# Sparse attention of a two-block transformer: four group turns become one unrolled stream of 64 steps

## The reference, cut to what matters

```python
def nsa_compressed(q, k, v, ...):      # 31 compressed keys and values per group
    s = einsum('bsghd,bngd->bghsn', q, kc) * NSA_SCALE
    p = masked_softmax(s, end[None, :] <= t[:, None])
    o = einsum('bghsn,bngd->bsghd', p, vc)
# selected blocks: top 16 of 8 blocks of 64 keys, so all of them, under the causal mask
# window: 512 keys back, with 512 tokens in all, so the causal mask alone
#   s = einsum(q, k) * NSA_SCALE ; p = masked_softmax(s, mask) ; o = einsum(p, v)
# the three outputs of a head are summed, each times its own gate per token and head
```

## Time and profile before

| | us |
|---|---|
| median of 3 runs (2740.66 to 2742.11) | 2741.51 |
| the profiled execution | 2737.46 |
| its span, first to last instruction | 2735.2 |
| PE busy | 2542.9 (93%) |
| POOL busy | 963.8 (35%) |
| ACT busy | 913.7 (33%) |
| DVE busy | 670.7 (25%) |
| sparse attention on PE, 1426.06 to 1798.09 | 372.0 |

### The profile page before, as it was taken

The page is one execution under the profiler, slowest core; times in us unless marked ns, Lnnn a source line. Parts: engine busy times, 40 slices in busy tenths (PEclk is TensorE's granted clock), DMA queues, the critical chain, the costliest instruction groups (busy, mean ns, idle before and its releaser), DMA issues.

```text
span 2735.2 us, 30881 instructions
## 1 busy us (share of the span) xinstructions
PE 2542.9 (93%) x11116; PEld 1937.5 (71%) x11116; DVE 670.7 (25%) x1619; ACT 913.7 (33%) x1579; POOL 963.8 (35%) x496
## 2 busy tenths in 40 slices
PE   6999999999899899999888888889799999899997
PEld 5888775766676688877576655657566667788776
DVE  1011211223232201121305345435521111301121
ACT  4322322345344333232313244333332223432232
POOL 3444452522523544445212210223322224244344
PEclk9999999999999999999967786889899999899999
DMA  3322234221111233223300100101112222123232
GB/s 130 99 93 92 87 106 140 88 66 62 62 54 61 70 93 99 92 85 102 114 22 29 35 27 8 35 31 54 39 48 91 81 86 89 57 94 100 77 97 89
DMA packets 72938, 204.00 MB, mean 75 GB/s; under 512 B 7185, under 2 KB 22033, under 8 KB 72337
## 3 DMA queue, kind: packets, MB, share of 16 engines
q1 hardware_dynamic: 69760, 191.92, 22.2%
q10 hardware_dynamic: 3088, 10.97, 1.1%
HBM read 199.71 MB, written 2.10 MB: 74 GB/s over the span
## 4 chain that ended last, share of the span: by engine, by line
PE 72%; issue 16%; DVE 5%; ACT 4%; POOL 3%; DMA 0%; DVEq 0%; ACTq 0%; POOLq 0%
PE bank L614 15%; PE bank L615 15%; PE bank L621 15%; PE bank L827 4%; PE bank L1047 3%; POOL parts L461 3%; PE bank L764 2%; PE bank L1267 1%; ACT parts L1526 1%; PE bank L660 1%; PE bank L607 1%; PE bank L609 1%; PE bank L608 1%; DVE hid L2056 1%; PE bank L1340 1%
## 5 line engine op out<-in xcount | busy, mean ns | idle before, releaser
L461 POOL TENSOR_TENSOR parts<-slot,parts 128x1024 fp32r<-128x1024 f32 (+2 forms) x344 | 761.4, 2215 | 1066.0 <-ACT parts L1526 1061.7
L614 PE MATMUL bank<-hhi,parts 128*128 128x512 f32 x1872 | 751.7, 402 | 35.8 <-POOL parts L461 24.8
L615 PE MATMUL bank<-hhi,parts 128*128 128x512 f32 x1872 | 739.0, 395 | 0.0
L1526 ACT ACTIVATE parts<-slot 128x1024 fp32r<-128x1024 f32 (+2 forms) x290 | 281.1, 971 | 840.0 <-PE bank L621 774.3
L621 PE MATMUL bank<-hlo,parts 128*128 128x512 f32 x1872 | 465.2, 390 | 0.0
L614 PEld LDWEIGHTS bank<-hhi,parts 128*128 128x128 f32 x1872 | 357.6, 191 | 136.3 <-POOL parts L461 32.0
L615 PEld LDWEIGHTS bank<-hhi,parts 128*128 128x128 f32 x1872 | 358.2, 191 | 76.8 <-issue 3.8
L621 PEld LDWEIGHTS bank<-hlo,parts 128*128 128x128 f32 x1872 | 351.1, 188 | 74.3 <-issue 1.4
L459 POOL TENSOR_TENSOR parts<-slot,lanes 128x1024 fp32r<-128x1024 f32 x54 | 104.2, 1929 | 451.9 <-PE bank L621 180.0
L2099 DVE TENSOR_TENSOR hid<-silu,bank 128x512 f32 (+1 forms) x66 | 45.4, 688 | 650.1 <-PE bank L621 630.2
L827 PE MATMUL bank<-hhi,parts 128*128 128x512 f32 x416 | 116.8, 416 | 3.0 <-POOL parts L461 3.0
(11 more groups left out here) (352 smaller groups left out, 3152.2 us busy)
## 6 DMA issues: line engine op xcount, KB each, us to landing
slot<-w SPq DMA_DIRECT2D x264, 512.0 KB, 3.4
slot<-w SPq DMA_DIRECT2D x88, 256.0 KB, 2.7
slot<-w SPq DMA_DIRECT2D x48, 448.0 KB, 3.3
hid<-w SPq DMA_DIRECT2D x8, 512.0 KB, 3.2
x<-xT ACTq DMA_DIRECT2D x1, 2048.0 KB, 10.5
hid<-headtab ACTq DMA_DIRECT2D x8, 256.0 KB, 3.9
big<-cmpw ACTq DMA_DIRECT2D x1, 2048.0 KB, 9.2
hid<-w SPq DMA_DIRECT2D x8, 256.0 KB, 2.6
```

Of the source, the lines that this page charges most:

```text
L461: pool.tensor_tensor(low, w, high.bitcast(F32), ALU.subtract).then_inc(splits, 1)
L614: pe.matmul(out, high[:, k, :], mhi[:, k, :], start=(start and k == 0), stop=False)
L615: pe.matmul(out, low[:, k, :], mhi[:, k, :], start=False, stop=False)
L1526: act.activation(parts[nth % 2][:, 0, 0:kt, :], slot[j][:, 0:kt, :], ACT.Copy).then_inc(highs, 1)
```

## The change

The four turns become one straight list for all groups, of 4 x 16 = 64 steps and three more to drain it.

- **Values.** The four value panels (96 matmuls of 128 columns in each turn) become one pass for all four groups at once: four transfers each bring two tiles of k of all four groups' value weights, and 4 x 24 matmuls of 512 columns sum into banks 0, 1, 2 and 7, with tokens stationary.
- **Weaving.** Three panels of group 0 and 20 matmuls of the value pass stand ahead of step 0. The other 76 value matmuls and the 9 query and key panels of groups 1 to 3 are cut into short runs and woven into the steps, up to two runs in a step (`FILL`, `V_FILL`): one after the scores, one after the transposes. Group 3's steps have none.
- **Compressed branch.** Scores, softmax and transposes of all four token blocks of a group are done in one piece: 8 x 4 matmul instructions ahead of the group's first step, DVE instructions four times as wide, one exponential, four transposes in the group's fifth step.
- **Smaller.** One reciprocal for both heads of a step instead of two; the DVE memsets (L2478) go; outputs alternate between banks 7 and 2; the copies L554 to L557 go, as do POOL's waits for banks 3 and 6 ahead of the first split; POOL splits 16 panels in a row, each after the panel two before it is done; ACT copies the values out in step 5 (four copies) ahead of that step's own work; keys and queries of odd groups have buffers of their own.

The steps keep their order on every engine and their distances: transposes two steps behind the scores, outputs at every fourth step. The diff, cut to its core:

```diff
+FILL = [(6, 0)] + [(3, 2 + (p < 2)) for p in range(12)] + [(4, 0)]
+V_FILL = [(8, 8)] * 4 + [(12, 0), (0, 0)] + [(5, 4)] * 8
...
-            pool.wait_ge(free[3], n.at("free3"))
-            pool.wait_ge(free[6], n.at("free6"))
...
-            split_turns(GROUPS, NSA, range(4), (-1, 0), group_gates)
+            for p in range(16):
+                split(p, p % RING, p - 1, load=1 + p // RING)
...
+            def sparse_values(q, a, b):
+                high, low = (parts[(3 + q) % 2][:, part, :, :] for part in range(2))
...
+                for m in range(a, b):
+                    t, j = (m // 4, m // 2 % 2) if m < 16 else ((m - 16) // 2, m % 2)
+                    at = (0, 1, 2, 7)[t]
...
+                    mm = pe.matmul(out, (hhi if m < 16 else hlo)[:, 2 * q + j, t * P:(t + 1) * P],
+                                   (low if m < 16 and m % 2 else high)[:, j::2, :],
+                                   start=(q == 0 and m < 16 and m % 4 == 0), stop=(q == 3 and m >= 16 and j == 1))
...
+            for c in range(3):
+                sparse_panel(c, 0, 24)
+            compressed_scores(0)
+            woven(0, 20, sparse_values)
+            panels_done, values_done = 3 * 24, 20
+            for s in range(STEPS + 3):
+                g, p = s // 16, s % 16
...
+                if s < STEPS:
+                    if p == 0 and g >= 1:
+                        compressed_scores(g)
+                    sparse_scores(s)
+                for nth in range(2):
+                    if s < 5:
+                        woven(values_done, fill[nth], sparse_values)
+                        values_done += fill[nth]
+                    else:
+                        woven(panels_done, fill[nth], sparse_panel)
+                        panels_done += fill[nth]
+                    if nth == 0:
+                        if s >= 6 and s % 4 == 2:
+                            sparse_out((s - 6) // 4)
+                        if 2 <= s < STEPS + 2:
+                            turn_sparse(s - 2)
+                if p == 4 and s < STEPS:
+                    turn_compressed(g)
...
+            for s in range(STEPS + 1):
+                if s < STEPS and s % 16 == 0:
+                    compressed_front(s // 16)
+                if s < STEPS:
+                    sparse_minima(s)
+                if s >= 1:
+                    sparse_probs(s - 1)
+                if s % 16 == 1:
+                    compressed_back(s // 16)
```

More of the change, by code:

```diff
@@ L1278, in _, with sparse_panel @@
             n.past(CMP)
-            def compressed_scores(i):
+            def sparse_panel(c, a, b):
+                p, out = c if c < 3 else c + 4, bank[c % 2][:, :]
+                high, low = (parts[p % 2][:, part, :, :] for part in range(2))
+                if a == 0:
+                    pe.wait_ge(splits, n.at("splits", p + 1))
+                    emptied(c % 2, earlier(c))
+                for m in range(a, b):
+                    k = m // 2 if m < 16 else m - 16
+                    mm = pe.matmul(out, (low if m < 16 and m % 2 else high)[:, k, :], (hhi if m < 16 else hlo)[:, k, :],
+                                   start=(m == 0), stop=(m == 23))
+                if b == 24:
+                    mm.then_inc(products, 1)
@@ new lines, in woven, with compressed_scores @@
+            def woven(first, count, piece):
+                while count:
+                    p, a = divmod(first, 24)
+                    b = min(24, a + count)
+                    piece(p, a, b)
+                    first, count = first + b - a, count - (b - a)
+            def compressed_scores(g):
+                for odd in range(2):
+                    emptied((3 * g + odd) % 2, earlier(3 * g + odd) + 1)
+                    emptied(4 + odd, 17 * g)
+                if g == 0:
+                    emptied(3)
+                for t in range(TT):
+                    for pair in range(2):
+                        for odd in range(2):
+                            half, at = slice(64 * odd, 64 * odd + 64), (2 * t + pair) * 32
+                            mm = pe.matmul(bank[4 + odd][:, at:at + CMP_N], q_of[g][half, pair, t * P:(t + 1) * P],
+                                           kc_of[half, g, :], start=True, stop=True)
+                            if t == TT - 1 and pair == 1:
+                                mm.then_inc(cscores, 1)
@@ new lines, in sparse_scores, with turn_sparse @@
+                    emptied(4 + odd, 17 * g + 1 + s % 16)
+                    pe.matmul(bank[4 + odd][:, 0:(row + 1) * P], q_of[g][half, pair, row * P:(row + 1) * P],
+                              k_of[g][half, br, 0:(row + 1) * P], start=True, stop=True).then_inc(scores, 1)
+            def turn_sparse(s):
+                pe.wait_ge(probs, n.at("probs", 2 * s + 2))
+                for odd in range(2):
+                    emptied((6, 3)[odd], s)
+                    for b in range(s % 4 + 1):
+                        mm = pe.transpose(bank[(6, 3)[odd]][:, b * P:(b + 1) * P],
+                                          exs[(2 * s + odd) % 4][:, b * P:(b + 1) * P], ident)
+                    mm.then_inc(turned, 1)
@@ L1966, in _ @@
+            n.past(NSA)
             for s in range(8):
@@ new lines, in sparse_minima @@
+            def sparse_minima(s):
+                width = (s % 4 + 1) * P
+                for odd in range(2):
+                    b, k = 4 + odd, (2 * s + odd) % 4
+                    dve.wait_ge(scores, n.at("scores", 2 * s + odd + 1))
+                    dve.tensor_tensor_reduce(scs[k][:, 0:width], bank[b][:, 0:width],
+                                             tables[:, K_CAUS + T - width:K_CAUS + T], 1.0, 3e38,
+                                             ALU.add, ALU.min, least[:, k:k + 1]).then_inc(free[b], 1)
```

362 lines of the change are left out of this document (170 added, 192 removed).

## The result

The median went from 2741.1 to 2628.8 us: a ratio of 0.959 [0.958, 0.961], 112 us. The forecast was 2648 with a range of 2620 to 2684, so the time lies inside it, 19 us under the likeliest value. The profiled execution took 2629.2 us with a span of 2627.4 (before 2735.2); the span is 107.8 us shorter.

The account below looks back on a forecast made before the run. PE was taken to bound the kernel. Values 49, other work at the high clock 36, head 6.6 and small ones 2 save 93.5 us: 2737.5 to 2644.0 profiled, with the median 4.05 above, 2648; range 2620 to 2684.

Parts of the forecast that it names:

- slow rival: Rival: PE's clock stays low in the steps; over 64 steps 95 us, over the runs 58; 140 us slower, 2788; 3%.
- The work at the high clock: PE's scores, transposes and outputs over the steps: 16 x 8.77 = 140.3 us if all at the high clock.
- Head: Stage start to step 0: PE no longer waits for POOL's first split, gain 6.6 us; 25.0 us to step 0.
- Steps without runs: The 23 steps with no woven matmuls: PE idles 0.46 us in each, 10.5 us.
- Borders and handover: Waits on PE: 3 us at each of three group borders, 2 for ACT's value copies; 11 us, bounds 5 and 22.
- POOL's holds: POOL's splits beside the steps lengthen DVE's scalings; a third of 22 us taken: 7 us, bounds 0 and 24.
- Drain: End of the step list, after the last scores: 6.5 us, paid once instead of four times.
- Cuts: Cutting matmuls into 77 runs woven into the steps: 0.05 us net each, 4 us, bounds 0 and 16.
- Clock: Loss to PE's low clock in the steps: 3 us for group 3, bounds 0 and 15.
- Nothing new is late: Rival: runs, residual waits, splits and clock cost nothing, borders 3, drain 5; 258.6 us in all, 2622; 22%.
- Weaving hides nothing: Rival: PE waits in the steps where it waited before; 16 us more than forecast, 2664; 9%.
- Held by POOL: Rival: DVE is held by POOL's splits (24) and the wide pieces at borders (22); 28 us more, 2676; 15%.

## Why the prediction was right, and where it was off

**Readings.** The trough of the clock line is in slices 21 to 27, not 24 to 29, and the slow rival's 58 us over the runs come to 56 (292 times 0.42 less 0.2266); nothing in the forecast hangs on either. The step lengths that were named as signs came out: 3.26 us in groups 1 and 2 where no split stands beside them (13.03 for four), and 2.41 in group 3.

**Values: right.** Forecast 71 to 21.8 us, measured 71 to 23.3, a gain of 48 for 49. The Trainium skill's figure (TensorE: Matmul & The Clock Gate, "Back-to-back issue gap") would have given 19; the trace disagrees, now in the changed kernel too.

**The work at the high clock: right in size, and not all of it clock.** Scores, transposes and outputs went from 176.3 to 137.8 us, where the sum had 140.3. In the kernel before with wide values they took 159.1, in the kernel after without its runs 158.3: so half of the 38 us came only with the runs in the steps. Part of that half isn't the clock. At the high clock a transpose record stands 0.144 us from the next without the runs and 0.116 with them, one of the scores 0.225 and 0.198. Priced so, an estimate, some 31 of the 38 us are the clock and 7.6 the closer records, a gain that the prediction had only as "the transposes beside them get shorter" within its 0.05 us a run.

**Head: right.** 24.6 us for 25.0, and 6.9 for 6.6 when done alone.

**The loop of steps was 16.7 us too long in the sum** (243.4 for 260.1). Its terms for idle time were all too long, and those for the cuts and the clock too short:

- Steps without runs: 10.5 forecast, 2.5 measured. I had taken 1.83 us of idle per four steps from a turn of the kernel before. In the pipeline four such steps have 0.82 and take 9.64 us instead of 10.08, as the timeline of the last group shows:

```profile
1661.17 1.10 PE L1373 MATMUL bank<-big 64*128 64x128 f32 x4 [0.20 <-DVE lanes L2551]
1662.77 0.88 PE L1382 MATMUL bank<-consts,ex 128*128 128x128 f32 x6 [0.49 <-DVE ex L2563]
...
1670.81 0.37 PE L1373 MATMUL bank<-big 64*128 64x128 f32 x1 [0.20 <-DVE lanes L2551]
```

- Waits left in woven steps: 3 forecast, none seen.
- Borders and handover: 11 forecast, 7.2 measured: 2.95 once, and 0.90 + 0.56 at each of three borders (4.3 by the sum of L1352's and L1373's waits). DVE's wide back, which I feared for 3 us of delay, is five instructions of 0.18 to 0.68 us, 2.4 in sum, and is hidden: the gaps of 2 to 4 us at each group's second and third step, which I had named as a sign, didn't come.
- POOL's holds: 7 forecast, 3.8 measured. The holds on DVE came as feared, 25 us of them; a step with runs hides not two thirds but five sixths.
- Drain: 6.5 forecast, 3.1 measured. The end at the high clock took 9.1 us from the last scores where the turn before took 12.0.
- Cuts: 4 forecast, some 5 measured. The 216 panel and 76 values matmuls inside the steps stand 0.274 us apart, not 0.2266. Outside the low stretches it is 0.280 for the panels' short runs and 0.244 for the values' longer ones, which is 12.8 us; the scores and transposes beside them gave 7.6 back.
- Clock: 3 forecast, some 7 measured, the one term that was clearly too small. 17 us of the steps are at the low level, in three stretches (after the handover at 1471, and directly behind the second and the third border), and none in the bare steps after that. The 7 us are the estimate described with the runs taken out; two traces without a stretch bear it out (1.6 us for the one at the handover, 2.7 for the one at the second border).

With the head and the compressed pieces (0.7 less) they come to 17.2 us less, and the stage is 17.3 under the forecast (287.1 in the measure used here, 269.8 found). The median is 19.3 us under it: the stage's 17.3, less 3 us by which the rest of the span was longer, 0.5 for what the execution takes beyond its span (2.3 us before, 1.8 after), and 4.5 more because I carried over the 4 us by which before's median stands above its profiled execution, while after's stands 0.5 below its own.

**Reciprocal: wrong.** What was "given back by waiting for both exponentials" was worth 5 to 8 us by the medians, through the clock. The step that failed: I weighed DVE's 0.16 us against the wait, and not what the loop of a bare step does to PE's clock.

**The rivals.** "Nothing new is late" (2622) was nearer than the forecast would have it: 2629 lies between the two, nearer to it. "Weaving hides nothing" was refuted: in the stage, weaving is worth 27 us. "Held by POOL" has the mechanism right and the price at a sixth. The slow clock did not come, but its edge was closer than the 3% made it look: four bare steps of 9.64 us keep 1.00, and in the version that adds a second reciprocal to them it falls three times. The Trainium skill's sentence that transposes don't count as PE activity in the same way (TensorE: Matmul & The Clock Gate, "Part 4: PE-mode transpose") is neither shown nor refuted by it: 20 transposes in 9.64 us went with 1.00, and nothing here tells why the slower steps fell.

**Open.** Whether the 3 us outside the stage are more than scatter; how exactly the runs' 15.7 us beyond the directly hidden ones split between refill and clock; and why behind a border or in the drain the clock sometimes falls and sometimes not. Behind the first border it fell without the splits, with more of them and with ACT's high parts, and not in after or its repeat. With one trace of each version but after, a single low stretch of 3.4 or 6.8 us can't be laid to an edit by its trace alone.

## What to carry to other kernels

Price a step that moves into a pipeline from the densest place where it ever ran, not from one where it waited: the terms for idle time were 21 us too long in sum, and 14 of these were carried over from the old order. If PE's clock is part of the bound, the steps that have nothing woven in are the place to save a few tenths of waiting, since there a second reciprocal of 0.16 us on DVE cost 5 to 8 us, while in woven groups the same edit cost nothing. Weaving independent matmuls into a latency-bound loop hides most of another engine's trouble too (25 us on DVE became 4 on PE). Cutting them into runs of 2 to 6 costs about 0.05 us a matmul, and here the instructions beside them gave more than half of it back. And where the clock moves by itself between executions of one kernel, look at which stretches were low before a difference of a few us is given to an edit.

## What was not expected of the hardware

- A 512-column matmul in a short run costs 0.280 us, in an uncut one 0.2266 to 0.235, and a 128-column one 0.11.
- Idle times of a few tenths do not show in PE's timeline, as the ends are modelled. In the unwoven steps it is 0.86 us from the start of 4 transposes to the scores behind them, of which the timeline shows 0.20 as idle; in the woven ones they take 0.36. A table of idle therefore understates what weaving hides: of the 27 us only 15 were idle, and the rest lay in such tails and in the clock.
- In after each of the three low stretches of the steps begins within 2 us behind a wait of PE (2.95, 0.90 and 0.56 us), and what it takes comes on top: 1.7 us less idle at the handover came with 3.2 us less time. But not every wait is followed by one: the same two waits at the first border, and 1.79 us in the drain, passed at the high clock in after.
- Low stretches come and go at the same places whatever the edit: all of the 4.5 us saved by leaving splits out went into two of them, and doubled high parts, which left PE's idle as it was, lengthened the profiled stage by 5.2 us, in the main by the same two.
- Two scalings in a row were held 4.16 us by two instructions of POOL; until now only one by one (1.76 us) had been seen.
